# The first block's two mixers: convolution norm placed beside the last attention steps, other counts of taps and jobs a step

## The reference, cut to what matters

```python
def conformer_conv(u, conv_w, conv_b, ln_g, ln_b):
    a, gate = jnp.split(u, 2, axis=-1)
    g = a * jax.nn.sigmoid(gate)
    y = lax.conv_general_dilated(g, conv_w[:, None, :], ...) + conv_b     # 31 taps, 512 channels
    return jax.nn.silu(layer_norm(y, ln_g, ln_b))

def merge_groups(o_attn, o_conv, beta_attn, beta_conv, w_o):
    o = jnp.concatenate([rms(o_attn) * beta_attn, rms(o_conv) * beta_conv], axis=-1)
    return o @ w_o

# per layer, for the tokens and (first layer only) for the context
sh1, s1, g1, sh2, s2, g2 = jnp.split((sc @ w_mod[l] + b_mod[l])[:, None, :], 6, axis=-1)
hx = modulate(x, sh1, s1)
q, k, v, u = split_cols(hx @ w_in[l])
...
x = x + g1 * merge_groups(o_attn, o_conv, beta_attn[l], beta_conv[l], w_o[l])
x = x + g2 * peer(modulate(x, sh2, s2), ...)
```

## Time and profile before

| | us |
|---|---|
| median of three runs | 3414.76 |
| lowest, highest | 3410.61, 3419.15 |
| the profiled execution | 3416.32 |
| its span | 3414.5 |

### The profile page before, as it was taken

The page is one execution under the profiler, slowest core; times in us unless marked ns, Lnnn a source line. Parts: engine busy times, 40 slices in busy tenths (PEclk is TensorE's granted clock), DMA queues, the critical chain, the costliest instruction groups (busy, mean ns, idle before and its releaser), DMA issues.

```text
span 3414.5 us, 51179 instructions
## 1 busy us (share of the span) xinstructions
PE 3153.6 (92%) x20321; PEld 2776.8 (81%) x20321; DVE 2463.3 (72%) x4809; ACT 1511.8 (44%) x2761; POOL 1008.0 (30%) x901
## 2 busy tenths in 40 slices
PE   6997999998999999999898999899999899877898
PEld 4654799998989888888655999899999898744897
DVE  2694479888887788888586788897888745485540
ACT  3454333736557333333444465584555442223430
POOL 0000046555655434442000246555555100000000
PEclk9998999999999999999989999999999999956999
DMA  6386346968879999998357577899999654401443
GB/s 216 107 288 200 105 146 236 334 237 302 284 269 345 381 360 367 361 365 325 105 166 235 197 256 273 281 371 374 375 373 384 209 173 125 140 1 62 136 149 110
DMA packets 372094, 830.04 MB, mean 243 GB/s; under 512 B 20848, under 2 KB 242064, under 8 KB 353296
## 3 DMA queue, kind: packets, MB, share of 16 engines
q1 hardware_dynamic: 274128, 470.32, 40.1%
q0 software_dynamic: 95360, 352.41, 28.3%
q10 hardware_dynamic: 2368, 4.05, 0.3%
HBM read 750.11 MB, written 76.55 MB: 242 GB/s over the span
## 4 chain that ended last, share of the span: by engine, by line
PE 72%; DVE 20%; ACT 4%; DMA 2%; issue 1%; POOL 0%; DVEq 0%; SPq 0%; ACTq 0%; POOLq 0%
PE ps L841 15%; PE ps L775 15%; PE ps L548 15%; PE ps L867 10%; PE ps L911 4%; DVE fr L1458 3%; DVE area L1458 3%; PE ps L820 3%; PE ps L612 3%; DVE area L1466 2%; PE ps L599 2%; PE ps L565 2%; DVE acc L1458 1%; ACT fr L1020 1%; DVE plain L1838 1%
## 5 line engine op out<-in xcount | busy, mean ns | idle before, releaser
L1458 DVE TENSOR_TENSOR fr<-ring,fr 128x1024 fp32r<-128x1024 f32 x621 | 767.1, 1239 | 510.9 <-ACT fr L1020 505.7
L1020 ACT CAST fr<-ring 128x1024 fp32r<-128x1024 f32 x678 | 705.9, 1046 | 664.9 <-PE ps L841 323.2
L775 PE MATMUL ps<-fr 128*128 128x384 f32 (+1 forms) x6144 | 935.6, 310 | 20.9 <-DVE fr L1458 20.9
L775 PEld LDWEIGHTS ps<-fr 128*128 128x128 f32 x6144 | 889.2, 192 | 28.2 <-DVE fr L1458 25.5
L841 PE MATMUL ps<-fr 128*128 128x512 f32 x2304 | 523.9, 390 | 3.2 <-DVE fr L1458 3.2
L548 PE MATMUL ps<-fr 128*128 128x256 f32 (+1 forms) x3312 | 482.5, 308 | 30.7 <-DVE fr L1458 30.7
L841 PEld LDWEIGHTS ps<-fr 128*128 128x128 f32 x2304 | 433.4, 188 | 93.5 <-ACT area L1268 3.5
L548 PEld LDWEIGHTS ps<-fr 128*128 128x128 f32 x3312 | 449.2, 195 | 62.9 <-DVE fr L1458 37.4
L867 PE MATMUL ps<-fr 128*128 128x192 f32 x3072 | 347.7, 275 | 3.5 <-DVE fr L1458 3.5
L867 PEld LDWEIGHTS ps<-fr 128*128 128x128 f32 x3072 | 346.5, 193 | 3.6 <-ACT fr L1020 3.6
L2172 POOL DMA_INDIRECT plain<-in_peer_v,area x192 | 270.7, 1410 | 257.3 <-DVE area L1466 166.8
(11 more groups left out here) (185 smaller groups left out, 3543.6 us busy)
## 6 DMA issues: line engine op xcount, KB each, us to landing
ring<-in_peer_uT SPq DMA_DIRECT2D x128, 1024.0 KB
ring<-in_peer_v SPq DMA_DIRECT2D x128, 1024.0 KB
ring<-in_w_mod SPq DMA_DIRECT2D x48, 1024.0 KB
ring<-in_w_ada SPq DMA_DIRECT2D x36, 1024.0 KB
w_scratch<-acc POOLq DMA_DIRECT2D x36, 1024.0 KB
g_scratch<-area POOLq DMA_DIRECT2D x128, 192.0 KB
area<-g_scratch POOLq DMA_DIRECT2D x64, 384.0 KB
area<-w_scratch POOLq DMA_DIRECT2D x16, 1536.0 KB
```

Source lines behind the costliest of these rows:

```text
L775: ins = e.matmul(o[:, 0:D], pairs[m][0], pairs[m][1], start=(m == 0), stop=(m == 23))
L1020: e.copy(hi, x).then_inc(act.after(("high", name)), 1)
L1458: return e.tensor_tensor(o, a, b, op).then_inc(dve.after(*labels), 1)
```

## The change

Five taps a step in the first mixer and eight in the second (`TAPS`), two jobs instead of one in the steps of `DOUBLE`, six such steps in the first mixer and four in the second. The jobs of the tail go down by as many: none stays in the first mixer's tail, two stay in the second's. Once the taps are done (`conv_step`, step 24 and step 15), every engine moves one stage of the convolution's norm forward per step; the stages are written as generators, and a `yield` is one step. What stages are left runs after attention. The projection takes the convolution half (groups 4 to 7) first.

SyncE and the constants:

```diff
+TAPS = (5, 8)
+
+DOUBLE = ((26, 28, 30, 32, 34, 36), (17, 18, 19, 20))
...
+def jobs_at(l, n):
+
+    return 2 if n in DOUBLE[l] else 1
...
+        b.jobs = sum(jobs_at(l, n) for n in range(b.at.steps))
+
+        b.conv_step = (124 + TAPS[l] - 1) // TAPS[l] - 1
...
-        jobs(M.mixers[l].at.steps)
+        jobs(M.mixers[l].jobs)
         for c0 in W4:
             columns(("W", ("o", l), c0), A["w_o"][l], c0)
             if c0 == 0:
-                jobs(3 * GAP)
+                jobs(l * GAP)
...
```

TensorE's mixer (`together` and `project` take the order of the groups as `parts`):

```diff
-        attend(b.at, lambda: mods(1))
...
+            yield
+            yield
+            o = bank(("mu", l), (dve, ("mu", l)))
+            for k in range(4):
+                w.wait_ge(dve, ("conv", l, k))
+            products(o[:, 0:Tq], [(M.c("ones"), b.y[:, k, 0:Tq]) for k in range(4)]).then_inc(pe.after(("mu", l)), 1)
+            yield
+            yield
+            yield
+            squares(("ln", l), 4, Tq, lambda k: M.ACC[:, k, 0:Tq])
+            yield
+            yield
+            yield
+            yield
+            yield
+            squares(("mg", l, 1), 4, Tq, lambda k: M.ACC[:, 4 + k, 0:Tq])
+
+        stages = conv_norm()
+
+        def side(n):
+            mods(jobs_at(l, n))
+            if n >= b.conv_step:
+                next(stages, None)
+
+        attend(b.at, side)
         kept.clear()
...
+        for _ in stages:
+            pass
+        squares(("mg", l, 0), 4, Tq, lambda k: M.ACC[:, k, 0:Tq])
+        mods(l * GAP)
         project(("o", l), W4, 1024, Tq, HR, lambda k: ("low", "h", ("mg", l, k // 4), k), lambda m: (dve, ("xo", l, m)),
-                n_first=2)
+                n_first=2, parts=(4, 5, 6, 7, 0, 1, 2, 3))
```

ScalarE's mixer, `conv_norm` from its first working line (four `yield` stand ahead of it):

```diff
+            squares(("ln", l), 4, lambda k: b.y[:, k, 0:Tq], lambda k: M.ACC[:, k, 0:Tq], lambda k: [("mean", l, k)])
+            yield
+            yield
+            root(("ln", l), b.rstd[:, 0:Tq], 512, Tq, [("mean", l, 3)], 1)
+            yield
+            yield
+            for k in range(4):
+                w.wait_ge(dve, ("lng", l, k))
+                e.activation(b.y[:, k, 0:Tq], b.y[:, k, 0:Tq], ACT.Silu, bias=M.v(f"ln_b{l}", k)).then_inc(
+                    act.after(("lnb", l, k)), 1)
+            yield
+            w.wait_ge(act, ("lnb", l, 3))
+            squares(("mg", l, 1), 4, lambda k: b.y[:, k, 0:Tq], lambda k: M.ACC[:, 4 + k, 0:Tq],
+                    lambda k: [("lng", l, 3)])
+            yield
+            yield
+            root(("mg", l, 1), b.rstd[:, 0:Tq], 512, Tq, [("lng", l, 3)])
+            yield
+            yield
+            rounded(("mg", l), 1, lambda k: b.y[:, k, 0:Tq], Tq, HR)
+
+        stages = conv_norm()
+
+        def side(n):
+            if n >= b.conv_step:
+                next(stages, None)
+            mods(jobs_at(l, n))
...
         first_weights(("o", l), W4, 1024, (0, 1), 2)
         root_table()
...
+        squares(("mg", l, 0), 4, lambda k: b.OT[:, k, 0:Tq], lambda k: M.ACC[:, k, 0:Tq],
+                lambda k: [("attended", b.at.tag)])
+        root(("mg", l, 0), b.rstd[:, 0:Tq], 512, Tq, [("mh", ("mg", l), 1, 3)])
+        mods(l * GAP)
+        rounded(("mg", l), 0, lambda k: b.OT[:, k, 0:Tq], Tq, HR)
```

VectorE's `merged`, which the second block uses too (all four gains, then all four low parts, where they were interleaved two behind), and its mixer's `conv_norm` (three `yield` ahead of its first working line):

```diff
+    def merged(tag, T, part, beta, rstd, HR):
         for h in range(2):
...
+            scaled(tag, h, T, lambda k: part(h, k), lambda k: beta(h, k), rstd)
+            lows(tag, h, T, lambda k: part(h, k), HR)
...
+            ts(mu, ps(("mu", l))[:, 0:Tq], 1.0 / 512, None, M_, None, ("mu", l))
+            last()
+            for k in range(4):
+                tt(b.y[:, k, 0:Tq], b.y[:, k, 0:Tq], mu, SU, ("mean", l, k))
+            yield
+            yield
+            yield
+            yield
+            inverse(("ln", l), b.rstd[:, 0:Tq])
+            for k in range(4):
+                stt(b.y[:, k, 0:Tq], b.y[:, k, 0:Tq], M.v(f"ln_g{l}", k), b.rstd[:, 0:Tq], M_, M_, ("lng", l, k))
+            yield
+            yield
+            yield
+            yield
+            yield
+            scaled(("mg", l), 1, Tq, lambda k: b.y[:, k, 0:Tq], lambda k: M.v(f"beta_conv{l}", k), b.rstd)
+            yield
+            yield
+            lows(("mg", l), 1, Tq, lambda k: b.y[:, k, 0:Tq], HR)
+
+        stages = conv_norm()
+
+        def side(n):
+            for _ in range(TAPS[l]):
                 next(tap, None)
-            mods(1)
+            if n >= b.conv_step:
+                next(stages, None)
+            mods(jobs_at(l, n))
 
         attend(b.at, side)
-        for _ in tap:
+        for n in range(len(b.at.todo) + b.at.rec_lag, b.at.steps):
+            mods(jobs_at(l, n))
+        for _ in stages:
             pass
...
         first_weights(("o", l), W4, 1024, 2)
...
+        scaled(("mg", l), 0, Tq, lambda k: b.OT[:, k, 0:Tq], lambda k: M.v(f"beta_attn{l}", k), b.rstd)
+        lows(("mg", l), 0, Tq, lambda k: b.OT[:, k, 0:Tq], HR)
+        mods(l * GAP)
```

More of the change, by code:

```diff
@@ L600, in squares, with together @@
         ins.then_inc(pe.after(("ss", tag)), 1)
-    def together(first, T, HR, low):
+    def together(first, T, HR, low, parts=range(8)):
         made = []
@@ L606, in together @@
             made.append((label, name, bank(label, reader), M.tile(name)))
-        for k in range(8):
+        for k in parts:
             w.wait_ge(dve, low(k))
@@ L624, in project @@
             name = ("w", tag, m)
-            w.wait_ge(dve, low(7))
+            w.wait_ge(dve, low(parts[-1]))
             w.wait_ge(*M.low(name))
@@ L960, in mix_second @@
         w.wait_ge(act, ("vt2",))
[L961 removed]
+        attend(M.at2, lambda n: next(scan, None))
         for _ in scan:
```

108 lines of the change are left out of this document (43 added, 65 removed).

## The result

The changed kernel takes 3449.32 us (median of four runs, 3446.19 to 3453.02) against 3416.95 for the kernel before in the same comparison (four runs, 3410.61 to 3421.45): a ratio of 1.0097, 95% interval 1.0074 to 1.0121. It is about 32 us slower; 3434 was forecast, and the measured median lies at the upper end of the range, 3449, and 0.3 us beyond it. The profiled execution of after took 3449.28 us, with a span of 3447.5 us against 3414.5.

What follows compares the result with a forecast made beforehand. TensorE was taken to bound the first mixer's 512-key steps and VectorE its 256-key steps. The terms 11.1 + 4 + 3.9 + 0.5 gave +19.5 us, forecasting 3434 us at the median, range 3407 to 3449.

Steps and rivals of the forecast that it cites:

- The bound: Before the change, TensorE bounds the first mixer's 512-key steps, with VectorE close behind, and VectorE bounds its 256-key steps.
- Part 1: First mixer's steps with taps: five taps make VectorE bound them all, so the norm can begin 11.3 us late.
- Part 2: First mixer, step 25 to the projection's third weight block: 96.0 us against 96.2 before, gains and costs cancelling.
- the walk: Step-by-step timing of first-mixer steps 25 to 36 and tail: 51.8 us of TensorE work, 2.9 and 11.6 of waits.
- Part 3: TensorE's clock in the first mixer: a low-clock stretch of three 256-key steps with taps, taken as +4 us.
- the 96.2: Measured us before the change from step 25 to the projection's third weight block in the first mixer.
- Rival C: Low TensorE clock through most 256-key steps with taps: 10.8 + 4 instead of 4, 3445 us or more; chance 0.16.
- A: Rival: no difference; the 11.6 us of first-mixer waits don't arise and the clock holds, 3419 us; chance 0.22.
- B: Rival: faster; no such waits, and ScalarE finishes weight blocks and convolution-half roundings before the last step, 3403 us; chance 0.12.
- Part 4: Second mixer: eight taps cost +3.3 us in the steps and the tail 0.6 more; taken +3.9, bounds -3 to +8.
- The +0.5: Second block's `merged` gives its first low parts two gains later: 0 to 0.8 us, taken +0.5.
- The rule beside a row: ScalarE table loads: trace shows 1.28 us without drain; the skill page's 1.38 drain per switch would add 5.5 us, 3440.

Runs made afterwards that it cites:

- second profile of after: The changed kernel run once more with nothing edited, to get another profile; one execution, 3445.16 us.

## Why the prediction was right in sign and too small

**The bound and Part 1** held. VectorE bounds all steps with taps, 4.23 and 3.96 us each, and step 25 is 11.7 us late (11.3 forecast). The fifth tap alone costs 5.7 us (by the interval 0.3 to 10), though, and that is no contradiction: Part 2 counts from step 25 and finds the steps behind it free of taps.

**Part 2, the walk** held where TensorE ran at full clock. In the second profile of after the mean's product ends 112.7 us behind the mark; the walk had 269.2 - 3.2 - 153.0 = 113.0. The waits, forecast against the first profile: step 28, 1.4 and 1.31; step 30, 1.9 and 1.87; Silu in step 32, 2.9 and 2.72; the second root in step 35, 1.8 and 2.21; the squares in step 34, 0.8 and 0.49. The 2.8 us for the reciprocal in step 32 didn't come: the reciprocal of 3.3 us at 303.55 lay beside a job that ran at the half clock. All waits of steps 25 to 36 are 10.1 us (9.2 in the second profile) for a forecast of 2.9 + 11.6 = 14.5. The convolution half's reciprocal did stand behind the last bias addition (339.77, then 339.84), as forecast; the wait ahead of the last squares was 8.46 us for a forecast of 8. From the last job row's end to the third weight block it was 31.4 us (340.66 to 372.04; 31.1 in the second profile), for a forecast of 29.7.

**Part 3, the clock, is the step that failed.** It gave +4 us, "a stretch of three such steps", with bounds up to about 15. TensorE's busy time in steps 25 to 36, the first line from the first profile and the second from the second, shows what the clock took; the walk had 51.8 us for the same instructions at full clock:

```profile
261.43:340.66 79.23, 69.17 (x439) 35.20 (x438) 16.11 (x49) 31.19 (x72) 0.00 (x0) 0.74 0.70 228
256.56:332.06 75.50, 66.29 (x439) 33.88 (x438) 17.97 (x55) 31.39 (x73) 0.00 (x0) 0.77 0.74 240
```

That is 17.4 and 14.5 us more of work, at a mean clock of 0.74 and 0.77, for the 4 us of Part 3. The half clock was granted for 41 and 34 us of these steps, so each microsecond of it made 0.42 us of work.

With it the first mixer adds up. It is late by Parts 1 and 2's 11.1 us, by the clock's 17.4 (14.5), less the 4.4 (5.3) us of waits that didn't come, and the tail is 1.7 (1.4) us longer. TensorE enters step 25 2.7 us later (1.2 earlier) than the walk's 101.7 us behind the mark. Together that is 28.5 (20.5) us, and 28.4 (20.5) were measured.

The mistake came in by a comparison: "Low-clock stretches stood in the tail before and are in the 96.2". They are, 30.7 us of them, 13.7 of these already in the last attention steps; but the walk set against the 96.2 has steps 25 to 36 at full clock, so Part 3 would have had to pay for all their low clock, and it paid for three steps with taps. The windows of 285 to 345 us, with the waits of 1.3 to 2.7 us that Part 2 itself puts there, ran at a clock of 0.79 and 0.70, and I had counted each wait once, as idle time.

The time at the half clock from 90 us on went from 30.7 us to 64.9 in the first profile and 47.8 in the second. These two are of one kernel and differ by 17.1 us of it and by 7.9 us of time, 0.46 us for each. The Trainium skill, "TensorE: Matmul & The Clock Gate", section "Terms", puts the penalty at throttled time x (1 - K/N), that is half of it at this level; the pair's 0.46 agrees.

One sum of Part 3 is also off: 3.04 us by 0.90 to 0.54 is 5.1, not 5.3, and the 0.54 is from the chain, where the same sum takes 0.61 in the timeline, the view of the 0.90. Two steps of after at the half clock, from 256.85 to 267.90, took 5.5 us each, so the 5.3 was near.

**Rival C** was the case that came, by size, though not as it was told. Its sign, a clock of 0.5 for over 20 us between 220 and 255, wasn't there: the stretch of 27.3 us began at 251.8, in the last two steps with taps, and lay mostly in the steps behind them. A and B fell: the waits arose, and ScalarE was not ahead.

**What the sum didn't separate.** Parts 1 and 2 priced the six jobs moved into the steps and the chain taken out of the tail as one comparison, 96.0 against 96.2, "what the norm gains in the tail, the jobs, products and waits that moved into the steps take". That hid that one of the two parts was nearly all loss: jobs in the tail had cost little, 1.4 us for six, since they lay in waits for ScalarE and VectorE, and moved to the steps they cost 9.6 us there, 8.2 us in the mixer and 15 us by the medians. I can show 8.2 of the 15 in the first mixer of that profile; 3.0 lie ahead of the first mark, and I leave the rest to the variation between executions.

**Part 4** was right in the steps and low in the sum. The chain through the second mixer of after, which answers to the earlier trace rows:

```profile
1812.69 0.61 DVE area L1643
...
1814.07 3.17 DVE area L1535 x8
...
1817.31 0.61 DVE area L1643
```

The eight taps give steps of 4.62 us (4.63 forecast) and make step 15 3.5 us late (3.3 forecast); the mixer as a whole is 5.5 to 8.4 us longer in every kernel that has the change there, for a forecast of 3.9 with bounds to 8, so the larger values lie just outside. In the second profile of after 1.7 of the 2.8 us more lie ahead of step 15, where the two executions run the same code. The +0.5 for the second block's `merged` wasn't measured by itself. The loads, costed at nothing with a bound of 3 us, cost nothing in after, whose steps are slow, 2.74 us where double jobs were tried alone and 2.20 us with the norm behind attention.

**The rule beside a row.** ScalarE's loads took 1.28 us and what followed started 0.01 to 0.02 us later, also between exponentials and root (297.33) and root and exponentials (305.75). The drain of 1380 ns that the Trainium skill, "ScalarE: Activation LUTs", section "What ACT_TABLE_LOAD costs", adds to each switch isn't seen in these rows, and the 5.5 us more that it would have made were not needed for the ledger above.

**What stays open:** why the clock falls in one execution at 94 us behind the mark and not in another with a wait of the same 1.39 us at that place; and whether taps and double jobs together cost more than each alone, as the 7.1 us of the medians say. More low clock would explain it (64.9 and 47.8 us against 23.9 and 27.3 with either undone), but no run held the clock fixed.

## What to carry to other kernels

Before moving work out of a stage with gaps, ask what lay in those gaps: six jobs that had been nearly free beside a serial chain of ScalarE and VectorE cost 8 us and more once they stood in steps that TensorE bounds. A serial chain in a tail is shortened better by taking a link out (a second root in a buffer of its own, 0.4% faster than before) than by laying it beside steps whose engines are full. A walk through the order gives waits to a few tenths, but every gap of 1 to 3 us that it puts on TensorE also has to be priced in granted clock, here 0.4 to 0.5 us for each microsecond at the lower level in which TensorE has work. A sum at full clock can't be set against a measured stretch that holds low clock.

## What the runs showed of the hardware that was not expected

- The clock fell to the half level behind single idle times of 1.39 us, with TensorE busy 39.4 of the 43 us around them, and stayed there for 27.3 us in which its only wait was 0.49 us. In another execution of the same kernel it didn't fall there, behind a wait of the same 1.39 us (250.72).
- Filling TensorE's idle time in ten steps didn't change the total time: the one profile has no low stretch of 27.3 us at 94.7 us behind the mark, and one of 30.7 us at 142.6.
- Executions of one kernel differ more than the medians of some kernels: 3417.70 to 3447.77 us with four taps, 3414.15 to 3435.37 for before with five. The difference between two profiles of the first was spread over the whole program, most of it in stages far from the change.
- A 1 MB piece stood on the chain with 7.81 us when it was asked for behind the first piece of `w_o` in the shortened tail; asked for three jobs earlier it caused no wait.
